# A two-model stack on one core: the first pair of chunks behind a norm in another order, and one modulation column moved behind the last add to x

## What is computed

```python
for layer in range(2):
    mod = (silu(c) @ ada_w[layer] + ada_b[layer]).reshape(B, 3, 3, D)     # shift, scale, gate
    h = rms_norm(x, norm_g[layer, 0]) * (1 + scale[0]) + shift[0]
    x = x + 0.5 * gate[0] * swiglu(h, ffn_w_in[layer, 0], ffn_w_down[layer, 0])
    h = rms_norm(x, norm_g[layer, 1]) * (1 + scale[1]) + shift[1]
    x = x + gate[1] * mixer(h)
    h = rms_norm(x, norm_g[layer, 2]) * (1 + scale[2]) + shift[2]
    x = x + 0.5 * gate[2] * swiglu(h, ffn_w_in[layer, 1], ffn_w_down[layer, 1])
```

## Time and profile before

| what | before |
|---|---|
| time, median of 3 runs | 3268.7 us |
| lowest and highest of the 3 | 3261.55 and 3279.51 us |
| span of the profiled execution | 3263.6 us |
| TensorE busy | 2987.7 us, 92% of the span |
| VectorE busy | 2250.3 us, 69% |
| ScalarE busy | 1376.3 us, 42% |
| chain that ended last | TensorE 84%, VectorE 9%, DMA 3%, ScalarE 3% |
| mean granted TensorE clock | 0.957 |

### The profile page before, as it was taken

The page is one execution under the profiler, slowest core; times in us unless marked ns, Lnnn a source line. Parts: engine busy times, 40 slices in busy tenths (PEclk is TensorE's granted clock), DMA queues, the critical chain, the costliest instruction groups (busy, mean ns, idle before and its releaser), DMA issues.

```text
span 3263.6 us, 48467 instructions
## 1 busy us (share of the span) xinstructions
PE 2987.7 (92%) x18636; PEld 2626.9 (80%) x18636; DVE 2250.3 (69%) x3214; ACT 1376.3 (42%) x1462; POOL 462.7 (14%) x244
## 2 busy tenths in 40 slices
PE   3999789999866699889999999999969999999999
PEld 3887478788755588669999998888759999988887
DVE  6886678856767655656978865566567978865565
ACT  3444444444452344444444444444434443444443
POOL 0310013011000011003870000000004860000000
PEclk9999689999988799889999999999989999999999
DMA  6785157846750255214556665677434556665676
GB/s 256 281 291 207 69 206 271 296 168 224 260 192 1 90 188 173 103 65 168 181 180 215 211 219 193 244 269 260 155 115 168 180 183 221 216 206 193 245 275 214
DMA packets 146921, 640.41 MB, mean 196 GB/s; under 512 B 12472, under 2 KB 46304, under 8 KB 90352
## 3 DMA queue, kind: packets, MB, share of 16 engines
q1 hardware_dynamic: 126960, 568.02, 49.5%
q10 hardware_dynamic: 19840, 70.79, 6.0%
HBM read 604.14 MB, written 34.62 MB: 196 GB/s over the span
## 4 chain that ended last, share of the span: by engine, by line
PE 84%; DVE 9%; DMA 3%; ACT 3%; issue 1%; SPq 0%; DVEq 0%; ACTq 0%
PE pp L465 24%; PE pp L467 12%; PE pp L809 8%; PE pp L810 7%; PE pp L811 7%; PE mz L875 6%; PE mz L877 6%; PE mz L878 6%; PE mz L851 3%; DMA raw<-expert_v 1%; DVE w_lo L1347 1%; ACT w_hi L974 1%; PE mz L455 1%; DVE ada_raw L1377 1%; DMA ada_raw<-ada 1%
## 5 line engine op out<-in xcount | busy, mean ns | idle before, releaser
L1347 DVE TENSOR_TENSOR w_lo<-raw,w_hi 128x2048 fp32r<-128x2048 f32 (+1 forms) x422 | 924.6, 2191 | 476.9 <-ACT w_hi L974 476.0
L974 ACT ACTIVATE w_hi<-raw 128x2048 fp32r<-128x2048 f32 (+1 forms) x486 | 894.2, 1841 | 553.4 <-DMA raw<-expert_v 362.7
L465 PE MATMUL pp<-hs,w_hi 128*128 128x512 f32 x2400 | 871.5, 407 | 39.1 <-DVE hs L1397 38.7
L467 PE MATMUL pp<-hs,w_lo 128*128 128x256 f32 x2400 | 680.0, 283 | 0.0
L465 PEld LDWEIGHTS pp<-hs,w_hi 128*128 128x128 f32 x2400 | 456.5, 190 | 169.9 <-issue 44.4
L809 PE MATMUL pp<-hs,w_hi 128*128 128x256 f32 x2048 | 585.8, 286 | 0.0
L810 PE MATMUL pp<-hs,w_hi 128*128 128x256 f32 x2048 | 580.3, 283 | 0.0
L811 PE MATMUL pp<-hs,w_lo 128*128 128x256 f32 x2048 | 580.2, 283 | 0.0
L1952 POOL TENSOR_TENSOR w_lo<-raw,w_hi 128x2048 fp32r<-128x2048 f32 x64 | 319.5, 5006 | 1098.7 <-ACT w_hi L974 1098.7
L467 PEld LDWEIGHTS pp<-hs,w_lo 128*128 128x128 f32 x2400 | 461.9, 192 | 1.0 <-issue 1.0
L875 PE MATMUL mz<-w_hi,w_split 128*128 128x512 f32 x1024 | 401.1, 392 | 11.2 <-DVE w_split L1719 11.2
(11 more groups left out here) (298 smaller groups left out, 3172.3 us busy)
## 6 DMA issues: line engine op xcount, KB each, us to landing
raw<-expert_u SPq DMA_DIRECT2D x128, 1024.0 KB, 4.9
raw<-expert_v SPq DMA_DIRECT2D x128, 1024.0 KB, 4.9
raw<-ffn_in SPq DMA_DIRECT2D x88, 1024.0 KB, 4.8
ada_raw<-ada ACTq DMA_DIRECT2D x120, 512.0 KB, 5.4
raw<-ffn_down SPq DMA_DIRECT2D x64, 704.0 KB, 5.5
raw<-out_w SPq DMA_DIRECT2D x16, 1024.0 KB, 4.8
raw<-hgrn SPq DMA_DIRECT2D x16, 1024.0 KB, 4.9
raw<-query SPq DMA_DIRECT2D x16, 1024.0 KB, 4.8
```

The costliest lines, as they stand in the source:

```text
L465: mm(outp, w_hi[:, slot, a:a + P], rhs[:, k0 + k].rearrange("p a t -> p (a t)"), start=(k0 + k == 0), stop=False, skip_group_check=True)
L467: last = mm(outp[:, 0:T], w_lo[:, slot, a:a + P], rhs[:, k0 + k, 0, :], start=False, stop=(k0 + k == last_k), skip_group_check=True)
L974: f(w_hi[:, slot, 0:n], raw[:, slot, 0:n], ACT.Copy).then_inc(hi_ready, 1)
L1347: v.tensor_tensor(w_lo[:, slot, 0:n], raw[:, slot, 0:n], w_hi[:, slot, 0:n].bitcast(F32), ALU.subtract)\
```

## The change

Two edits. In the first, the 32 units of the first pair behind a norm (two chunks, four output tiles) get another order on TensorE. `first_pair` does, for k = 0 to 3, one unit of each of the four tiles; then the remaining four k of chunk 0's two tiles, then those of chunk 1's. It waits for both chunks' `w_lo` at its start, and it waits for `hs_ready` at each k once. On ScalarE and VectorE, in the same opening pair, `split_next` stands ahead of `take_cross` and `add_halves`. In the second, in the last pair of each ffn_down phase, the modulation column of j = 1 stands behind the last `add_to_x`.

```diff
+            def first_pair(ph, n):
+                pair, half = ph.pair0, ph.pair0 % 2
+                def part(j, t, k):
+                    return tile_product(pp[:, j, t], 2 * half + j, t * KD + k, hs, k, 1, KD - 1)
+                pe.wait_ge(evac_done, ph.evac0)
+                pe.wait_ge(lo_ready, 2 * pair + 2)
+                for k in range(KD // 2):
+                    pe.wait_ge(hs_ready, KD * n + k + 1)
+                    for j in range(2):
+                        for t in range(2):
+                            part(j, t, k)
+                for j in range(2):
+                    for k in range(KD // 2, KD):
+                        if j == 0:
+                            pe.wait_ge(hs_ready, KD * n + k + 1)
+                        for t in range(2):
+                            last = part(j, t, k)
+                    last.then_inc(w_used, 1)
...
@@ ScalarE, products
+                    opening = isinstance(rp, int) and rp == 0
                     for j in range(2):
                         e = ph.evac0 + 2 * rp + j
+                        if opening:
+                            split_next(ph, rp, pair, half, lap, j)
                         take_cross(ph, e, j, 2 * pair + j + 1)
-                        split_next(ph, rp, pair, half, lap, j)
+                        if not opening:
+                            split_next(ph, rp, pair, half, lap, j)
                         load_modulation(ph, 2 * rp + j + 1, 1 - j)
...
@@ VectorE, ffn (projections alike)
+                        if opening:
+                            split_next(ph, rp, pair, half, j)
                         add_halves(both[:, j], e, j)
-                        split_next(ph, rp, pair, half, j)
+                        if not opening:
+                            split_next(ph, rp, pair, half, j)
...
@@ VectorE, ffn, the loop over ffn_down
+                    closing = isinstance(rp, int) and rp == KD - 1
                     for j in range(2):
                         split_next(ph, rp, pair, half, j)
-                        modulation(ph, rp, j)
+                        if j == 0 or not closing:
+                            modulation(ph, rp, j)
                     dve.wait_ge(w_used, 2 * pair + 2)
                     add_to_x([pp[:, half, 0:1, a * T:(a + 1) * T] for a in range(2)], a_gate[:, n, bass.ds(rp, 1)],
                              xT[:, bass.ds(rp, 1), :], KD * halves_of[n] + rp)
+                    if closing:
+                        modulation(ph, rp, 1)
```

More of the change, by code:

```diff
@@ L469, in tile_product @@
                 return last
+            def first_pair(ph, n):
[16 more added lines that the diff above has]
+                    last.then_inc(w_used, 1)
             def products(ph, n):
[L473 to L477, removed]
+                first_pair(ph, n)
+                for rp, pair, half, lap in pairs_of(pe, ph.part(1, ph.pairs - 1)):
                     for j in range(2):
@@ L481, in products @@
                         for t in range(2):
-                            first = isinstance(rp, int) and rp == 0 and j == 0 and t == 0
-                            last = tile_product(pp[:, j, t], 2 * half + j, t * KD, hs, 0, KD, KD - 1,
-                                                tile_of_h if first else None)
+                            last = tile_product(pp[:, j, t], 2 * half + j, t * KD, hs, 0, KD, KD - 1)
                         last.then_inc(w_used, 1)
@@ L992, in products @@
                 load_modulation(ph, 0, 0)
-                for rp, pair, half, lap in pairs_of(act, ph):
+                for rp, pair, half, lap in itertools.chain(pairs_of(act, ph.part(0, 1)), pairs_of(act, ph.part(1, ph.pairs - 1))):
+                    opening = isinstance(rp, int) and rp == 0
                     for j in range(2):
                         e = ph.evac0 + 2 * rp + j
+                        if opening:
+                            split_next(ph, rp, pair, half, lap, j)
                         take_cross(ph, e, j, 2 * pair + j + 1)
-                        split_next(ph, rp, pair, half, lap, j)
+                        if not opening:
+                            split_next(ph, rp, pair, half, lap, j)
                         load_modulation(ph, 2 * rp + j + 1, 1 - j)
@@ L1363, in projections @@
             def projections(ph):
-                for rp, pair, half, lap in pairs_of(dve, ph):
+                for rp, pair, half, lap in itertools.chain(pairs_of(dve, ph.part(0, 1)), pairs_of(dve, ph.part(1, ph.pairs - 1))):
+                    opening = isinstance(rp, int) and rp == 0
                     for j in range(2):
+                        if opening:
+                            split_next(ph, rp, pair, half, j)
                         add_halves(pj[:, bass.ds(4 * rp + 2 * j, 2), :], ph.evac0 + 2 * rp + j, j)
-                        split_next(ph, rp, pair, half, j)
+                        if not opening:
+                            split_next(ph, rp, pair, half, j)
                         modulation(ph, rp, j)
```

## The result

| what | before | changed |
|---|---|---|
| time, median | 3268.7 us (5 runs, 3261.55 to 3279.51) | 3253.1 us (5 runs, 3246.58 to 3255.04) |
| ratio to before, 95% interval | | 0.9942 [0.9928, 0.9956] |
| span of the profiled execution | 3263.6 us | 3251.3 us |
| mean granted clock | 0.957 | 0.957 |
| the eight first pairs together | 114.1 us | 105.8 us |

The median went down by 15.6 us; the ratio says 14 to 24 us. The profiled execution went down by 12.3. The forecast was 10.0 us, 0.3%. The size is thus about 0.5%, on the edge of what the prediction called distinguishable, and its best value is larger than the forecast in both sets; the interval of the second, 9 to 21 us, still holds 10.0.

A forecast was written before the change was run, and what follows sets the result against it. TensorE, busy 92% of 3263.6 us, was taken to lose time at norms: waiting for the norm chain, and at h's pace or half clock in first pairs. Gains 6.1 + 3.9 = 10.0 us took 3268.7 to 3258.7 us, range 3246 to 3271.

The forecast's parts named there:

- What bounds the stretch: First pair behind a norm: h tiles come every 0.77 us, units take 0.35 us at full clock, 0.67 at half.
- C: Half-speed part of a first pair, worked out from the granted clock: mean 4.8 us, together 38.5 over eight pairs.
- Part one: New unit order in eight first pairs: each takes 11.2 + 0.478 C, together 108.0 instead of 114.1 us, gain 6.1.
- Rival 2: In the first pairs the clock returns sooner, C 3.1 us in all: total gain 16.6, time 3252.1 us; chance 0.12.
- What the new order delays: Chunk 0 finishes after 24 units, not 16; its slot's reload, its banks and new waits were forecast to cost nothing.
- 7.3 us chain behind chunk 0: In feed-forwards, chunk 0's cross copy to chunk 1's add; TensorE needs it 8.4 us later, cover 1.1 us, no wait.
- Part two: Modulation column behind the last add in three ffn_down phases: 1.3 us hidden at each, gain 3.9 us.
- square, sum and root follow 1.33 us sooner: Norm chain behind ffn_down: adds start earlier, so the root is ready at 649.40 instead of 650.73.
- The tables' slack: At the norm behind ffn_down, VectorE finishes column and tables before the reciprocal needs it, with 0.1 us to spare.
- The rule against it: Skill page's clock rule, read as: changing PSUM bank with every unit keeps TensorE at half speed for the whole first pair.
- Rival 3: Changing banks holds the clock down: all 32 units at 0.67 us, 7.2 us more a pair, 3322 us; chance 0.04.

The follow-up runs named there:

- both sets: Two sets of timed runs of the same changed kernel against the kernel before: ratios 0.9942 and 0.9955, medians 3253.1 and 3254.4 us.

## Why the prediction came out as it did

- **What bounds the stretch.** Right: h at 0.77 us a tile, units at 0.35 or, at half speed, 0.64 us (0.67 in the prediction), and the clock decides between them. The old order is unmoved by a full clock, 14.1 to 14.3 us with C = 0, and the new order takes 11.4.
- **Part one, 11.2 + 0.478 C.** Right in form, small in size: forecast 6.1 us, in the trace 8.3 us (114.1 to 105.8), timed alone 9.5 with 5 to 14 as its interval. Two terms were off. A unit at half speed takes 0.64 us in a row, not 0.67: the pair of rows that I took, 659.68 to 660.35, follows a late tile of h. With 0.64 the slope is 0.453, worth 38.5 x 0.025 = 1 us. And C was not the same: in the two traces of the old order 38.5 and 37.4 us over eight pairs, in the seven of the new order without extra matmuls 33.6 to 36.2, so about 3 us shorter, worth 1.4 us; single pairs scatter from about 3 to 6 us in both, so with two traces of the old order this is likely rather than shown. Rival 2 named it; it came true by about a fifth of its range, not in full. Why TensorE's closer work would end C sooner I have not tested by itself.
- **What the new order delays.** Right. The changed kernel has no wait at units 32, 48 and 64. The 7.3 us chain behind chunk 0 took 7.3: chunk 0 ends at 67.28 (unit 24), its cross copy is at 67.48, and chunk 1's add ends at 74.54; unit 48 starts at 75.60, a cover of 1.1 us, as forecast. The splits back in place show what lay under the cover that the edit made: 2 us a norm.
- **Part two, the column.** The mechanism was right and its size was small: 3.9 us forecast, 5.6 us timed alone [1.6 to 9.5], which does not tell the two apart, 4.7 in the one pair of traces and 6.5 by the sites of all traces. The mis-sized step is "square, sum and root follow 1.33 us sooner", taken as if they and the flips kept their durations. On average they got faster by 0.5 us a site: with a shorter wait for x the clock is more often still up when the sums come. In the pair of traces that is 1.0 us at norm 1, where sums and flips ran at 1.00 instead of 0.60, 0.2 at norm 4 and nothing at norm 3. I priced the clock in the first pair and forgot it in the chain ahead of it. The other 0.3 us a site, ahead of the adds, looks like chance.
- **The tables' slack**, 0.1 us to spare: about right, with the sign turned. They now end 0.1 us behind the root, and would be the next thing in the way.
- **The rule against it.** Units that change bank every 0.35 us ran at a granted clock of 1.00 for whole pairs (446.10:457.52 above). Rival 3 is refuted here. The page that the prediction names for it, "TensorE: Matmul & The Clock Gate" of the Trainium skill, section "A second HAM failure mode: psum-queue depth-cycling", ties the falling clock to TensorE's brief idle times, and not to the change of bank as the prediction's use of it did. By the traces the pairs in the new order have no idle time of TensorE over 0.1 us.
- **The total.** 10.0 forecast, 12.3 in the trace, 15.6 in the medians. The trace's 12.3 is 8.3 for the pairs, 4.7 for the three column sites (from the last product to the first one behind the norm: 10.5, 8.8, 9.2 us before, 8.5, 7.6, 7.7 after), and 0.7 given back elsewhere. The remaining 3 us lie in the choice of executions: a span is 1.8 us shorter than the time of its own run, so the profiled run of before lay 3.3 us under its median, while that of the changed kernel is its median. That the medians come within 1 us of rival 2 (3252.1) is chance: its C of 3.1 us in every pair is not what the traces show (34.5 over eight, not 24.8).

## What to carry to other kernels

Where an engine waits tile by tile for another, count the independent units that each arriving tile could feed, and take just as many as cover its pace: two did what four did, and left every release in its old place. Before pricing such a reordering, read the granted clock in that very stretch: here it took two thirds of the gain, and filling TensorE's idle time ahead of the stretch with matmuls of no use gave that back, while the same filling gave the old order next to nothing. And a step moved out of a chain ahead of TensorE can be worth more than its length, if the shorter idle time leaves the clock up more often; here that was 0.5 us a site on 1.33, and a single trace could not have shown it.

## What the runs showed of the hardware

A unit at full clock has one of two paces, 0.3533 or 0.3467 us, and nearly always keeps it for a whole phase (an ffn_in, an ffn_down); the attn phase lies between, at about 0.352. Starts of units on TensorE in the changed kernel, behind norm 2 (17 units in 6.01 us) and behind norm 3 (15 units in 5.20 us), both at a granted clock of 1.00:

```profile
451.91 0.40 PE L465 MATMUL pp<-hs,w_hi 128*128 128x512 f32 x1
...
457.92 0.40 PE L465 MATMUL pp<-hs,w_hi 128*128 128x512 f32 x1
...
653.47 0.39 PE L465 MATMUL pp<-hs,w_hi 128*128 128x512 f32 x1
...
658.67 0.39 PE L465 MATMUL pp<-hs,w_hi 128*128 128x512 f32 x1
```

From unit 32 to ffn_down's last product the feed-forward behind norm 2 takes 180.0 us, all at the first pace; the one behind norm 3 takes 177.6 us, with ffn_in at the second pace and ffn_down at the first. Which pace a phase has differs from one execution to another. The kernel has 3360 such units, so the two paces are up to 22 us apart. In the twelve traces the time above the second pace comes to 7.8 to 19.3 us, in the two of the changed kernel to 11.0 and 7.8, whose spans are 7.0 us apart. It can thus make a good part of the scatter of the timed runs (3260.6 to 3279.7 us for the kernel before), but no run shows that it does. What sets the pace is open.
